# Turning the operands of two narrow projections round, and spreading the second layer's modulation blocks

## The reference

```python
mod_l = (s_lat @ w_mod[l] + b_mod[l])            # 6 x 1024 values: shift, scale, gate, twice
a_l = _rmsnorm(h, norm_mix[l]) * (1.0 + sc_m) + sh_m
u_l = (a_l @ w_in[l]).astype(jnp.float32)        # 15 blocks of 256 columns, and 32 narrow columns:
...                                              # per head a time step, decay and beta of both directions
dtf = jax.nn.softplus(dt_f + dt_bias[0])
fwd = (xs * dtf[..., None], dtf * a[0], bm, cm)
...
h = h + g_m * (y_l @ w_out[l])
f_l = _rmsnorm(h, norm_ffn[l]) * (1.0 + sc_f) + sh_f
scores = jax.nn.sigmoid(jnp.dot(h, router_w))    # 64 experts
_, idx = lax.top_k(scores + router_bias, TOP_K)  # 8 of them per token
```

## Time and profile before

| | |
|---|---|
| three runs | 3105.01, 3105.82, 3105.00 us, median 3105.01 |
| profiled execution | 3093.14 us, its span 3091.0 us |
| mean granted TensorE clock | 0.899 of 2.4 GHz |
| TensorE busy | 2580.1 us (83%) |
| VectorE, ScalarE, GpSimd busy | 1242.6, 580.2, 567.8 us |
| read from HBM | 552.37 MB |

### The profile page before, as it was taken

The page is one execution under the profiler, slowest core; times in us unless marked ns, Lnnn a source line. Parts: engine busy times, 40 slices in busy tenths (PEclk is TensorE's granted clock), DMA queues, the critical chain, the costliest instruction groups (busy, mean ns, idle before and its releaser), DMA issues.

```text
span 3091.0 us, 44060 instructions
## 1 busy us (share of the span) xinstructions
PE 2580.1 (83%) x14904; PEld 1751.5 (57%) x14905; DVE 1242.6 (40%) x2705; ACT 580.2 (19%) x980; POOL 567.8 (18%) x561
## 2 busy tenths in 40 slices
PE   6999778778676999999996789777786699999985
PEld 3337667767563555555553445676675455555553
DVE  3432566666443222222222443456664322222223
ACT  1125211212110111111111115312211011111111
POOL 0000222222004222222221000122220222222221
PEclk8999878878778999999998799878788799999998
DMA  5643000000142899999997243100003499999994
GB/s 224 236 156 99 1 1 1 1 1 1 44 195 84 309 362 352 351 341 337 361 347 231 96 163 94 33 1 1 1 1 109 181 349 370 366 365 367 375 361 150
DMA packets 170445, 573.17 MB, mean 185 GB/s; under 512 B 31966, under 2 KB 81446, under 8 KB 131398
## 3 DMA queue, kind: packets, MB, share of 16 engines
q1 hardware_dynamic: 143718, 520.29, 44.4%
q0 software_dynamic: 26592, 51.11, 6.8%
HBM read 552.37 MB, written 53.53 MB: 196 GB/s over the span
## 4 chain that ended last, share of the span: by engine, by line
PE 55%; DVE 18%; DMA 12%; issue 6%; DVEq 3%; ACT 2%; POOLq 1%; POOL 1%; ACTq 1%; SPq 0%
PE ps L1552 50%; DMA featT<-ffn_rows,idx_in 8%; DVE R L983 7%; PE ps L1556 5%; DMA R<-in_exp_down 2%; DVE featT L983 1%; DVE R L989 1%; DMA R<-in_w_mod 1%; ACT L758 1%; ACT R L758 1%; POOLq L674 1%; DVE R L1299 1%; DVEq L980 1%; POOL slots L650 1%; DVE R L1198 1%
## 5 line engine op out<-in xcount | busy, mean ns | idle before, releaser
L1552 PE MATMUL ps<-R 128*64 128x256 f32 (+5 forms) x10224 | 1618.8, 382 | 165.6 <-DVE R L983 88.3
L1552 PEld LDWEIGHTS ps<-R 128*64 128x64 f32 (+2 forms) x10224 | 1052.8, 178 | 600.7 <-issue 319.3
L983 DVE TENSOR_TENSOR R<-R,ps 128x256 f32<-128x256 f32 (+2 forms) x364 | 216.2, 594 | 676.5 <-ACT R L758 500.8
L758 ACT ACTIVATE R<-ps 128x256 f32<-128x256 f32 (+2 forms) x387 | 164.2, 424 | 1163.6 <-PE ps L1552 1142.1
L1552 PE MATMUL ps<-featT,ring 128*128 128x512 f32 (+1 forms) x768 | 318.5, 573 | 1.6 <-ACT R L758 0.8
L1552 PEld LDWEIGHTS ps<-featT,ring 128*128 128x128 f32 x768 | 150.2, 199 | 165.6 <-issue 159.2
L1556 PE MATMUL ps<-ident,featT 128*128 128x128 f32 x1120 | 161.5, 290 | 91.0 <-DMA featT<-ffn_rows,idx_in 56.9
L986 DVE TENSOR_SCALAR R<-ps,idx_out 128x512 f32<-128x512 f32 x128 | 96.1, 751 | 300.1 <-PE ps L1552 300.1
L1556 PEld LDWEIGHTS ps<-ident,featT 128*128 128x128 f32 x1120 | 127.1, 146 | 147.1 <-issue 58.3
L640 POOL TENSOR_TENSOR R<-R,lev 128x512 f32<-128x512 f32 x112 | 142.5, 1272 | 346.1 <-PE ps L1552 218.7
L992 DVE COPY R<-ps 128x256 f32<-128x256 f32 (+2 forms) x282 | 154.3, 547 | 115.5 <-PE ps L1556 97.8
(11 more groups left out here) (183 smaller groups left out, 1540.2 us busy)
## 6 DMA issues: line engine op xcount, KB each, us to landing
R<-in_exp_gate SPq DMA_DIRECT2D x128, 1024.0 KB, 7.9
R<-in_exp_up SPq DMA_DIRECT2D x128, 1024.0 KB, 11.2
R<-in_exp_down SPq DMA_DIRECT2D x128, 1024.0 KB, 15.9
R<-in_w_mod SPq DMA_DIRECT2D x48, 1024.0 KB, 7.7
ring<-in_w_in SPq DMA_DIRECT2D x30, 1024.0 KB, 6.0
ring<-in_w_out SPq DMA_DIRECT2D x8, 1024.0 KB, 5.3
ffn_sum_odd<-zero SPq DMA_DIRECT2D x6, 512.0 KB, 7.3
ffn_rows<-X SPq DMA_DIRECT2D x6, 512.0 KB, 2.7
```

Source lines behind the costliest of these rows:

```text
L758: do(C.activation(out_, in_, func, **kw), name)
L983: do(V.tensor_tensor(out_, a, b, op), name)
L1552: return MM(out_, lhsT, rhs, start=start, stop=stop)
```

## The change

**Small projection and router turned round.** Now the weights are stationary (128 by 32, or 128 by 64) and `featT` moves with all its tokens (512; 256 in the router of layer 1). The eight channel tiles go to four groups of 32 PSUM partitions in turn (two groups of 64 in the router), so that each group holds a partial sum over two (four) tiles, with tokens along the free axis. ScalarE copies the bank into `X`, and a second, small set of multiplications with `X` stationary and a stack of identities moving (`sel4`, `sel2`) adds the groups and turns the result back to tokens on partitions: one per chunk. For the small projection that set stands behind block 0; for the router it follows at once. VectorE makes `sel2` and `sel4` in the head. `zero` shrinks from 128 to 32 columns to make room, and the zeroing DMA repeats it 32 times instead of 8 per row.

**Modulation.** `MOD_AT` says how many tiles stand after a half, `TURN_AT` after which block a part is gathered. In layer 0 both come out as before, but VectorE's `mod_add` moves from ahead of the copies of the next block (3, 6) to behind those of block 2 and 5. In layer 1 the 16 tiles, formerly two after each half of blocks 0, 1, 3 and 4, now stand one or two at a time after the halves of blocks 0 to 2 and 4 (second half) to 7 (first half). Part 4 is gathered after block 3 (before: 2), part 5 after block 8 (before: 5), where ScalarE's `mod_row` stands behind its copy of block 8, and `mod_add` behind the first long step of the forget gates.

```diff
+MOD_AT = ({(3 * p + n, half): 2 for p in range(3) for n in range(2) for half in range(2)},
+          {(0, 0): 1, (0, 1): 2, (1, 0): 1, (1, 1): 2, (2, 0): 1, (2, 1): 1,
+           (4, 1): 1, (5, 0): 1, (5, 1): 2, (6, 0): 1, (6, 1): 2, (7, 0): 1})
+TURN_AT = ({2: 1, 5: 2, 8: 3}, {3: 4, 8: 5})
...
-                    sp.dma_start(acc_odd[tk(c), :].rearrange("p (a b) -> p a b", b=P),
-                                 zero[:, :].unsqueeze(1).to_broadcast([P, KT, P])).then_inc(S["acc_zeroed"], 16)
+                    sp.dma_start(acc_odd[tk(c), :].rearrange("p (a b) -> p a b", b=32),
+                                 zero[:, :].unsqueeze(1).to_broadcast([P, DM // 32, 32])).then_inc(S["acc_zeroed"], 16)
...
+                wait("sm_ps", 1, l)
+                f(X[:, 0, 0:TOK], ps[:, 3, :], ACT.Identity, "cum_act")
                 for n in range(N_CONV):
-                    if n % 3 == 2 and n // 3 < len(MOD_UNDER[l]):
-                        mod_row(MOD_UNDER[l][n // 3])
+                    if n in TURN_AT[l]:
+                        mod_row(TURN_AT[l][n])
...
                 u_copy(N_CONV + 1)
-                if len(MOD_UNDER[l]) > 2:
-                    mod_row(MOD_UNDER[l][2])
+                mod_row(TURN_AT[l][N_CONV + 1])
...
                 wait("lg_ps", 1, l)
+                f(X[:, 0, P * c0(l):TOK], ps[:, 0, P * c0(l):], ACT.Identity, "lg_exp")
+                wait("lg_ps", 2, l)
                 f(scor[:, cs, :], ...)
...
+            tt(sel2[:, :], ident[:, 0:NE], ident[:, NE:P], ALU.add)
+            tt(sel4[:, :], sel2[:, 0:32], sel2[:, 32:64], ALU.add)
...
                 for n in range(N_CONV):
-                    if n % 3 == 0 and 0 < n <= 3 * min(len(MOD_UNDER[l]), 2):
-                        mod_add(MOD_UNDER[l][n // 3 - 1])
                     wait("u_ps", n + 1, l)
...
                     dve.drain().then_inc(S["u_dve"], 1)
+                    if n in TURN_AT[l]:
+                        mod_add(TURN_AT[l][n])
...
-                for c in range(NT):
-                    for k in range(KT):
-                        ins = mm(ps[:, 3, 32 * c:32 * c + 32], featT[:, k, tk(c)], wsm[:, k, :], k == 0, k == KT - 1)
+                for k in range(KT):
+                    g = k % MG
+                    ins = mm(ps[g * 32:(g + 1) * 32, 3, :], wsm[:, k, :], featT[:, k, :], k < MG, k >= KT - MG)
                 ins.then_inc(S["sm_ps"], 1)
...
                     ins.then_inc(S["u_ps"], 1)
+                    if n == 0:
+                        wait("cum_act", 1, l)
+                        for c in range(NT):
+                            ins = mm(ps[:, 3, 32 * c:32 * c + 32], X[:, 0, tk(c)], sel4[:, :])
+                        ins.then_inc(S["sm_ps"], 1)
...
+                for k in range(KT):
+                    g = k % 2
+                    ins = mm(ps[g * NE:(g + 1) * NE, 0, P * live[0]:], rw[:, k, :], featT[:, k, P * live[0]:], k < 2, k >= KT - 2)
+                ins.then_inc(S["lg_ps"], 1)
+                wait("lg_exp", 1, l)
                 for c in live:
-                    for k in range(KT):
-                        ins = mm(ps[:, 0, c * NE:(c + 1) * NE], featT[:, k, tk(c)], rw[:, k, :], k == 0, k == KT - 1)
+                    ins = mm(ps[:, 0, c * NE:(c + 1) * NE], X[:, 0, tk(c)], sel2[:, :])
                 ins.then_inc(S["lg_ps"], 1)
```

More of the change, by code:

```diff
@@ L110, in only_live @@
     return kind in ("hq", "gate") or (kind == "conv" and i in (3, 4))
+MOD_AT = ({(3 * p + n, half): 2 for p in range(3) for n in range(2) for half in range(2)},
+          {(0, 0): 1, (0, 1): 2, (1, 0): 1, (1, 1): 2, (2, 0): 1, (2, 1): 1,
+           (4, 1): 1, (5, 0): 1, (5, 1): 2, (6, 0): 1, (6, 1): 2, (7, 0): 1})
+TURN_AT = ({2: 1, 5: 2, 8: 3}, {3: 4, 8: 5})
 def in_steps(l):
+    q = 0
     for n in range(N_IN):
-        part = MOD_UNDER[l][n // 3] if n // 3 < len(MOD_UNDER[l]) else None
         for half in range(2):
             yield "half", n, half
[L119 to L123, removed]
+            for _ in range(MOD_AT[l].get((n, half), 0)):
+                yield "mod", MOD_UNDER[l][q // KT], q % KT
+                q += 1
+        if n in TURN_AT[l]:
+            yield "turn", TURN_AT[l][n], 0
 def late(ap, w, d):
@@ L168, in build @@
         selP = sb("selP", [P, MG, 2])
+        sel2 = sb("sel2", [P, NE])
+        sel4 = sb("sel4", [P, 32])
         stage = sb("stage", [P, 2, P])
@@ L304, in build @@
         more = sb("more", [1, NBLK * NE], I32)
-        zero = sb("zero", [P, P])
+        zero = sb("zero", [P, 32])
         ps = ctx.enter_context(nc.psum_tensor("ps", [P, 8, 512], F32))
@@ L331, in build @@
             ("u_ps", N_IN), ("u_dve", N_CONV), ("u_act", N_IN - N_CONV), ("conv_out", CT), ("silu_out", CT),
-            ("sm_ps", 1), ("sp_x", 1), ("sp_exp", 1), ("sp_done", 1), ("cum_ps", 1), ("cum_dve", 1),
-            ("cum_act", 1), ("small_done", 1),
+            ("sm_ps", 3), ("sp_x", 1), ("sp_exp", 1), ("sp_done", 1), ("cum_dve", 1),
+            ("cum_act", 2), ("small_done", 1),
             ("l2_sq", 4), ("l2_ps", 4), ("l2_act", 4), ("l2_done", 4),
@@ L1103, in _ @@
                 dve.wait_ge(S["bc_loaded"], (l + 1) * 16 * BC_DMAS)
-                wait("sm_ps", 1, l)
+                wait("sm_ps", 2, l)
                 cp(sm[:, :, :].rearrange("p c f -> p (c f)"), ps[:, 3, 0:32 * NT])
@@ L1140, in _ @@
                 dve.drain().then_inc(S["hg_dve"], 1)
-                if len(MOD_UNDER[l]) > 2:
-                    mod_add(MOD_UNDER[l][2])
-                wait("cum_ps", 1, l)
+                mod_add(TURN_AT[l][N_CONV + 1])
+                wait("sm_ps", 3, l)
                 for d in range(2):
@@ L1168, in _ @@
                 dve.drain()
-                wait("cum_act", 1, l)
+                wait("cum_act", 2, l)
                 tt(wdt[:, :, :, :], dt_[:, :, :, :], wend[:, :, :, :], ALU.mult)
@@ L1390, in _ @@
                 norm_turn(1, l)
-                wait("lg_exp", 1, l)
+                wait("lg_exp", 2, l)
                 do(V.memset(blank[:, :, 1:2], 0.0))
@@ L1657, in _ @@
                             mm(ps[:, 2, 48 * d:48 * d + 48], tri[:, d, :], da[:, :, d, :])
-                        mm(ps[:, 2, 96:192], ones[:, :], da[:, :, :, :].rearrange("p c d h -> p (c d h)")).then_inc(S["cum_ps"], 1)
+                        mm(ps[:, 2, 96:192], ones[:, :], da[:, :, :, :].rearrange("p c d h -> p (c d h)")).then_inc(S["sm_ps"], 1)
                     if n in (N_CONV + 4, N_CONV + 5):
@@ L1851, in _ @@
                 wait("grow_sb", len(conds(l)), l)
-                for c in live:
-                    for k in range(KT):
-                        ins = mm(ps[:, 0, c * NE:(c + 1) * NE], featT[:, k, tk(c)], rw[:, k, :], k == 0, k == KT - 1)
+                for k in range(KT):
+                    g = k % 2
+                    ins = mm(ps[g * NE:(g + 1) * NE, 0, P * live[0]:], rw[:, k, :], featT[:, k, P * live[0]:], k < 2, k >= KT - 2)
                 ins.then_inc(S["lg_ps"], 1)
                 wait("lg_exp", 1, l)
+                for c in live:
+                    ins = mm(ps[:, 0, c * NE:(c + 1) * NE], X[:, 0, tk(c)], sel2[:, :])
+                ins.then_inc(S["lg_ps"], 1)
+                wait("lg_exp", 2, l)
                 for n in range(2):
```

2 lines of the change are left out of this document (1 added, 1 removed).

## The result

| | before | changed | |
|---|---|---|---|
| median of four runs | 3105.41 us (3105.0 to 3106.82) | 3062.44 us (3061.84 to 3063.58) | ratio 0.9869, interval 0.9857 to 0.988 |
| profiled execution | 3093.14 us, span 3091.0 | 3061.84 us, span 3059.6 | 31.4 us off the span |
| mean granted clock | 0.899 | 0.904 | |

The runs lost 43.0 us, the traced spans 31.4; 34.1 was forecast.

The account below looks back on a forecast made before the run. TensorE was taken to bound the kernel, holding 55% of the chain. Gains of 13.5 + 12.4 + 5.7 + 2.5 = 34.1 us take the profiled 3093.14 to 3059; runs, less another 11.9 above it, 3071, range 3061 to 3083.

Parts of the forecast that it names:

- Small projection: Input stages: 16 records of 128x32 by 512 take 3.6 us, gaining 10.0 us in layer 0 and 9.0 in layer 1.
- Clock behind it: Block 0's first half: 1.4 us low-clock loss kept in each layer, gaining 0.6 us in layer 0 and 1.4 in layer 1.
- Turn back: Behind block 0 in each layer: four small multiplications, 8 records, cost 1.0 us on the path.
- VectorE's gaps of layer 0: Layer 0 input stage: gaps of 1.69 and 2.18 us, tiles waiting for `mod_add`, both go: 3.9 us gained.
- Router: Layer 0: long records 6.2 us, whole 8.2 against 13.9, gain 5.7 us; layer 1: 3.4 against 5.9, gain 2.5.
- Gather of part 4: Layer 1, after block 3: TensorE waits 2.5 us for ScalarE's row, plus 0.8 clock loss, 3.3 us given back.
- The stop at the sum of the decays: Layer 1: sum starts 18.7 us after block 8, TensorE stands still about 7 us, stage end pays 5.9 us.
- Sum of the four places: Both input stages and both routers: 13.5 + 12.4 + 5.7 + 2.5 = 34.1 us off the profiled execution.
- (a): Rival, layer 1: the late gather costs nothing because ScalarE gets round it; 3065 us, chance 0.06.
- (b): Rival, projections and routers: column groups overlap less with `featT` moving, by the 0.79 share; 3075 us, chance 0.07.
- (c): Rival, projections and routers: groups don't overlap, reading different channel tiles from the same buffer; 3103 us, chance 0.04.
- (d): Rival, layer 1: after the 7 us stop the clock stays low through blocks 10 to 14; 3114 us, chance 0.03.

Follow-up runs that it names:

- e7: The changed kernel with all eight channel tiles of small projection and router summed in one column group; ratio 0.9921 to the kernel before, 3071.54 us.
- e2: The changed kernel with the modulation (tiles, gathers, `mod_add`) back at its old places, only small projection and router turned; ratio 0.9903 to the kernel before.
- e6: The changed kernel with layer 1's old modulation table, `mod_add` left at its new place; ratio 0.986 to the kernel before, 3051.17 us.
- e4: The changed kernel with another layer 1 table, part 4 gathered after block 2 and part 5 after block 6; ratio 0.9861 to the kernel before, 3048.19 us.
- e1: The kernel before, unedited, traced and timed again; ratio 0.9997, span 3086.1 us.
- e8: The changed kernel, unedited, traced and timed again; ratio 0.9887 to the kernel before, 3060.53 us.
- e9: The kernel before with only `zero` shrunk to 32 columns and its DMA in 32 pieces per row, buffers unmoved; ratio 0.9997, 3092.35 us.
- e10: The kernel before with the smaller `zero` and an unused 96-column tile shifting later buffers by 384 bytes; ratio 1.0021, 3100.28 us.
- e3: The changed kernel with small projection and router as before, so only the modulation changed; ratio 0.9996 to the kernel before.

## Why the prediction was right, and where it was off

The time and the way were right; the range, 3061 to 3083, held 3062.4 at its lower end. For the profiled execution 3059 was forecast and 3061.84 came: near, because two misses cancel, as told below. For the runs 3071 was forecast, 8.6 us too much: it adds the 11.9 us by which the kernel before stood above its own trace, and in the changed kernel that distance was 0.6. By the steps:

- **Small projection.** 3.6 us each forecast; 3.38 and 3.64 came. With one group (e7) it took 8.66 in layer 0: turning alone brought the step from 13.8 to 8.7, and the groups brought the rest. The time also hangs on when the clock rises: the same 16 records took 1.92 us in layer 0 in e2 and e6.
- **Clock behind it.** 1.4 us of loss kept in each layer; none in layer 0, 1.1 in layer 1. Layer 0's 2 us over the forecast are mostly this and the projection. In the kernel before the clock stayed at 1.2 GHz through the 64 short records; behind the 16 long ones it was at 2.4 in layer 0, and in layer 1 it rose only at about 1714 us, 6 us after their start.
- **Turn back, VectorE's gaps of layer 0.** 1.0 and 3.9 forecast; 1.08 (67.95 to 69.03) and 3.9 came.
- **Router.** The step that was mis-sized: 6.2 us for layer 0's long records, with the clock rising in the middle, and it was 3.65, at 2.4 GHz from the first. I had read the low clock off the old router's own end, which the change takes away with the router itself: in other traces it fell only under the old router (last section). In all eight traces of a turned router with two groups the stretch took 5.92 us; in the five with the old one it took 12.8 to 14.4.
- **Gather of part 4.** Wait 2.5 forecast, 2.80 came; clock loss 0.8 against 1.7.
- **The stop at the sum of the decays.** 18.7 us after block 8 forecast, 19.0 came. The wait was 9.16 and not 7; the rows themselves give 18.7 less 1.79 for ScalarE's row, 0.9 for the gather and 7.14 for block 9, 8.9, so that the 7 was a slip, on which the price does not rest. The price at the end of the stage: 5.9 forecast, 4.8 and 5.7 measured (e4).
- **Sum of the four places**: 34.1 forecast, 38.8 came (35.9 by e1's and e8's traces).
- **Not seen at all**: the shifted buffers. I priced `zero`'s smaller pieces and `sel2`'s VectorE work and asked of neither where it pushes the buffers behind it. It took 7 to 8 us (e9 and e10) and hid in two expert loops of 1375 us together. Between the first two traces the expert parts took 8.4 us: 3.5 are the second loop, where every trace shows the shift; most of what is left is the first loop, 741.1 for 736.5, which varies from trace to trace (735.4 to 739.1 us with nothing shifted). This loss more than cancels the 4.7 by which the places did better than forecast, which is why the trace's 31.4 lies so near 34.1. That nearness is luck.
- **The signs.** By the prediction's own list it would be wrong if the expert loops changed by more than 3 us, and they did: the first by 4.6 in the first pair of traces, the second by 3.5. The exp came 5.5 us after the router's first multiplication and not 8, and the wait at `tri` was above its 6 to 8. The stretch from layer 1's small projection on shrank by 12.1, within 7 to 18; counted from block 0, as the list has it, it shrank by 3.1, and the forecast's own terms give no more than 3.4 there.
- **Rivals.** (a) fell: the stop is there and had its price. (b) and (c) fell by e7: 3.7 times for four groups at the full clock, 1.93 for two. (d) fell: behind the stop only 2.5 us were lost in block 10, and the clock was up again at 1874 to 1876 us.
- **Open.** Why the kernel before ran at 3105 in its first session and at 3092.6 to 3095.0 in three later ones, while the changed kernel stood at 3062.4 and 3060.5. The time's own gain is therefore 34 to 43 us, by session.

The change's second half did not do what it looks like. Its new place of `mod_add` gave 4.3 us in layer 0 and 5.3 in layer 1 (e2 and e6). The even table itself is a loss of 6.5 us in the stage (5.3 by e8's trace) against the old table with the same `mod_add` (e6). e4's table, which is neither even nor old, is 3.4 better still by its stage (200.8 and 204.2), though the times of e4 and e6 can't be told apart (0.9861 and 0.986).

## What to carry to other kernels

A product with a narrow result (32 or 64 columns) and many tokens wants the narrow side stationary, the tokens moving, and its partial sums in column groups; summing and turning them back costs one more copy and a few short multiplications. With these paid it was worth 8 to 9 us of 13 to 14 with 512 tokens, and 2.8 of 6.2 in the router with 256. Before work is spread evenly for the transfers' sake, look at who waits for the last piece: here the last gather had to be early for the sum of the decays, and evenness removed only one wait of 2.3 us with its clock loss. And a tile that is added in the middle of the allocations moves the buffers behind it: put it last, or time and trace a padded twin before the difference is ascribed to anything else.

## What the runs showed of the hardware that was not expected

384 bytes of unused SBUF ahead of the large buffers made the whole program 7.9 us slower (3092.35 to 3100.28). In the traces 4.1 us of that stand in the second expert loop, which moves 3 MB of weights per expert at a DMA share of 0.93 to 0.95, and there the same 33600 weight packets took 81.4% of the engines' 600 us for 80.8%. The weights land in `R`, which was shifted; the gathered tokens land in `featT`, which was not. Whether the address of the weight slots alone does it, and which addresses are good, was not tried.

At the same place behind the same transposes, the turned router had the clock at 2.4 GHz from the first record on in eight traces of eight. The old one had it at 1.2 GHz for all or most of its 64 short records, though TensorE was busy without a break. In e1's trace the clock was at 2.4 GHz when the old router began, at 893.45 us, and fell under it (stretch, length, busy time of TensorE, its weight loads, VectorE, ScalarE and GpSimd, then granted clock, DMA share, GB/s):

```profile
893.50:898.50 5.00, 5.00 (x31) 5.00 (x32) 0.00 (x0) 0.00 (x0) 0.00 (x0) 0.66 1.00 415
898.50:903.50 5.00, 5.00 (x26) 5.00 (x25) 0.00 (x0) 0.00 (x0) 0.00 (x0) 0.50 1.03 433
```

The windows of e3 show the same fall, and so do those of layer 1 in all five traces of the old router. In the traces of the kernel before, e9 and e10 the clock of layer 0 had fallen already 2 us ahead of the router, under the transposes; no run shows why there. So part of what turning gains is the clock: under long records it stayed up.
